# Unrolling the expert loop, a shorter threshold search and a reordered last tile in a Hyena/retention/expert-choice layer kernel

## The reference, cut to what matters here

```python
def trunk_layer(x, mod, p, s0_f, s0_b, use_rope):
    sh1, sc1, g1, sh2, sc2, g2 = mod
    h = rmsnorm(x, p["norm1_g"]) * (1.0 + sc1) + sh1
    out, s_f, s_b = mixer(h, p, s0_f, s0_b, use_rope)   # ends with merged @ w_out
    x = x + g1 * out
    h = rmsnorm(x, p["norm2_g"]) * (1.0 + sc2) + sh2
    x = x + g2 * ec_moe(h, p)
    return x, s_f, s_b

def ec_moe(h, p):
    xt = h.reshape(T, D)
    aff = softmax(xt @ p["w_router"])                   # 16 experts
    cap = (2 * T) // N_EXPERTS
    vals, idx = lax.top_k(aff.T, cap)                   # each expert takes its tokens
    xs = xt[idx]
    hid = silu(xs @ w_e_gate) * (xs @ w_e_up)
    ye = (hid @ w_e_down) * vals[..., None]
    return zeros.at[idx].add(ye)
```

## Time and profile before

| what | value |
|---|---|
| runs, median (lowest to highest) | 3529.71 us (3528.85 to 3532.29), 3 runs |
| the profiled execution, its own time | 3532.37 us |
| its span, first to last instruction | 3530.5 us |
| mean granted TensorE clock | 0.949 of full |
| busy: TensorE / VectorE / ScalarE / GpSimd | 91% / 46% / 36% / 10% |
| output phase's last row done | about 2091 us after the start |
| threshold search | about 2100 to 2155 us |
| experts on TensorE | about 2195 to 3510 us |

### The profile page before, as it was taken

One profiled execution on the slowest core, in us unless ns is written; L12 is line 12 of the kernel. 1 busy time (PEld: TensorE's weight loads), 2 busy tenths in 40 slices (PEclk: granted clock), 3 DMA queues, 4 the chain that ended last, 5 costly groups with the idle time before them and its releaser, 6 DMA issues. The chain is left out here.

```text
span 3530.5 us, 53171 instructions
## 1 busy us (share of the span) xinstructions
PE 3219.0 (91%) x19287; PEld 2754.7 (78%) x19287; DVE 1614.5 (46%) x3031; ACT 1283.2 (36%) x1955; POOL 356.0 (10%) x313
## 2 busy tenths in 40 slices
PE   7589999799889699999979963999999999999996
PEld 2278888789745689989978852989888889888995
DVE  5333232433346442323225546655555555555555
ACT  4544443323233031222124431444444444434445
POOL 1011111000034100000000001011111111111112
PEclk9799999899999799999999975999999999999998
DMA  8533332422299751422134431455555555555557
GB/s 336 194 118 101 114 112 84 142 64 66 67 348 353 237 181 56 130 93 96 55 128 149 159 135 61 162 204 190 177 190 181 177 173 169 169 170 182 200 204 279
DMA packets 281627, 565.64 MB, mean 160 GB/s; under 512 B 22296, under 2 KB 161432, under 8 KB 277289
## 3 DMA queue, kind: packets, MB, share of 16 engines
q1 hardware_dynamic: 257023, 503.83, 40.8%
q0 software_dynamic: 15456, 54.88, 5.3%
q10 hardware_dynamic: 8976, 4.46, 0.4%
HBM read 434.44 MB, written 128.64 MB: 159 GB/s over the span
## 5 line engine op out<-in xcount | busy, mean ns | idle before, releaser
L71 PE MATMUL experts_bank<-experts_xT_high,experts_w_high_gu 128*128 128x272 f32 x2048 | 604.3, 295 | 20.1 <-issue 15.0
L73 PE MATMUL experts_bank<-experts_xT_high,experts_w_low_gu 128*128 128x272 f32 x2048 | 596.4, 291 | 0.0
L72 PE MATMUL experts_bank<-experts_xT_low,experts_w_high_gu 128*128 128x272 f32 x2048 | 592.6, 289 | 0.0
L71 PEld LDWEIGHTS experts_bank<-experts_xT_high,experts_w_high_gu 128*128 128x128 f32 x2048 | 388.8, 190 | 33.4 <-issue 27.3
L72 PEld LDWEIGHTS experts_bank<-experts_xT_low,experts_w_high_gu 128*128 128x128 f32 x2048 | 389.9, 190 | 4.3
L73 PEld LDWEIGHTS experts_bank<-experts_xT_high,experts_w_low_gu 128*128 128x128 f32 x2048 | 389.0, 190 | 0.0
L2858 DVE TENSOR_TENSOR experts_w_low_gu<-experts_w_raw_gu,experts_w_high_gu 128x1024 fp32r<-128x1024 f32 x256 | 303.3, 1220 | 20.4 <-ACT experts_w_high_gu L2664 20.3
L2664 ACT ACTIVATE experts_w_high_gu<-experts_w_raw_gu 128x1024 fp32r<-128x1024 f32 x256 | 257.6, 1047 | 19.0 <-DMA experts_w_raw_gu<-in_w_stream 18.8
L71 PE MATMUL merge_pg<-merge_hT_high,merge_w_gates_high 128*128 128x436 f32 (+1 forms) x640 | 231.8, 362 | 13.2 <-DVE merge_hT_low L2015 13.2
L72 PE MATMUL merge_pg<-merge_hT_low,merge_w_gates_high 128*128 128x436 f32 (+1 forms) x640 | 231.3, 361 | 0.0
L73 PE MATMUL merge_pg<-merge_hT_high,merge_w_gates_low 128*128 128x436 f32 (+1 forms) x640 | 230.9, 361 | 0.0
(11 more groups left out here) (383 smaller groups left out, 6534.1 us busy)
## 6 DMA issues: line engine op xcount, KB each, us to landing
experts_w_raw_gu<-in_w_stream SPq DMA_DIRECT2D x256, 512.0 KB
experts_w_raw_d<-in_w_stream SPq DMA_DIRECT2D x128, 512.0 KB, 6.5
filters_wm<-in_w_mod SPq DMA_DIRECT2D x12, 2048.0 KB, 11.9
merge_hT<-scratch_hT SPq DMA_DIRECT2D x32, 436.0 KB, 6.7
scratch_h<-out_row SPq DMA_DIRECT2D x17, 520.0 KB, 2.7
tokens_x<-in_xs SPq DMA_DIRECT2D x17, 512.0 KB, 5.2
scratch_hT<-tokens_hT SPq DMA_DIRECT2D x17, 512.0 KB, 4.4
scratch_qkT<-tokens_qkT SPq DMA_DIRECT2D x17, 512.0 KB, 2.8
```

Of the source, the lines that this page charges most:

```text
L71: pe.matmul(out, lhs[0], rhs[0], start=start, stop=False)
L72: pe.matmul(out, lhs[0], rhs[1], start=False, stop=False)
L73: return pe.matmul(out, lhs[1], rhs[0], start=False, stop=stop)
```

## The change

Three parts. (1) In `experts` the loop is gone: all 16 experts are written out on TensorE, ScalarE, VectorE and GpSimd. (2) In the search the next candidates are formed from the step itself, beside the threshold and not behind it; the three counts over 16 elements become one comparison of 48 elements and one reduction; shifting the bits is moved behind the counts; TensorE waits only for `seg`, and VectorE's wait for the other constants is moved behind the search. (3) In the output phase the last tiles have another order: tile 16's gate product and residual sum are moved ahead of tile 15's copy on VectorE, its norm ahead of tile 14's softmax on ScalarE and VectorE; `pr` has a bank for each parity, so that router t waits for the exponential of t-2; tile 16 has a row slot of its own. Inside the loop of the output phase the order is the same as before. The diff, cut:

```diff
-        row = sb("row", [P, 2, ROW])
+        row = sb("row", [P, 3, ROW])
...
-        pr = pb("pr", [P, NE])
+        pr = pb("pr", [P, 2, 512])
...
-        VB = counted("dve_rows", ["t1", "x", "rstd", "h2a", "h2", "hT"])
+        VA, VB = counted("dve_sums", ["t1", "x"]), counted("dve_rows", ["rstd", "h2a", "h2", "hT"])
...
+        def slot(t, h):
+            return 2 if isinstance(t, int) and t == NT - 1 else h
...
                 def router(t, h):
                     pe.wait_ge(VB.sem, VB.at(t, "hT"))
                     pe.wait_ge(AB.sem, AB.at(t, "hT"))
-                    pe.wait_ge(AR.sem, AR.at(t - 1, "ex"))
+                    pe.wait_ge(AR.sem, AR.at(t - 2, "ex"))
...
-                for t in range(LOOP, NT):
-                    if t + 2 < NT:
-                        front(t + 2, t % 2, (t + 2) // 2)
-                    router(t, t % 2)
-                    if t + 1 < NT:
-                        turn(t + 1, (t + 1) % 2)
+                front(NT - 1, 0, (NT - 1) // 2)
+                router(NT - 3, 0)
+                turn(NT - 2, 1)
+                router(NT - 2, 1)
+                turn(NT - 1, 0)
+                router(NT - 1, 0)
...
             @block.scalar
-                for t in range(LOOP + 1, NT + 1):
-                    if t < NT:
-                        back(t, t % 2, t // 2, t + 2 < NT)
-                    router(t - 1, (t - 1) % 2)
+                norm(NT - 2, 1)
+                turned(NT - 2, 1)
+                norm(NT - 1, 0)
+                router(NT - 3, 0)
+                router(NT - 2, 1)
+                turned(NT - 1, 0)
+                router(NT - 1, 0)
...
             @block.vector
-                for t in range(LOOP + 1, NT + 1):
-                    if t < NT:
-                        back(t, t % 2, t // 2, int(t == NLAT), t + 2 < NT)
-                    router(t - 1, (t - 1) % 2)
+                last, k = NT - 1, (NT - 1) // 2
+                total(last - 1, 1, k - 1, 0)
+                norm(last - 1, 1, k - 1, 0)
+                total(last, 0, k, 1)
+                turned(last - 1, 1)
+                largest(last - 2, 0)
+                norm(last, 0, k, 1)
+                router(last - 2, 0)
+                largest(last - 1, 1)
+                router(last - 1, 1)
+                turned(last, 0)
+                largest(last, 0)
+                router(last, 0)
...
         def experts(eng, body):
-            with eng.Fori(0, LOOP // 2, 1) as i:
-                for h in range(2):
-                    body(i * 2 + h, h, i, True, True)
-            for e in range(LOOP, NE):
+            for e in range(NE):
                 body(e, e % 2, e // 2, e + 1 < NE, e + 2 < NE)
...
-                for dst, src in ((seg, d["seg"]), (caps[:], d["caps"]), (slot[:], d["slot"])):
+                sp.dma_start(seg, d["seg"]).then_inc(lds, 16)
+                for dst, src in ((caps[:], d["caps"]), (slot[:], d["slot"])):
                     sp.dma_start(dst, src).then_inc(ldc, 16)
...
-                pe.wait_ge(ldc, 80)
+                pe.wait_ge(lds, 16)
...
                 for j in range(3):
+                    v.memset(cand[:, :, j:j + 1], (j + 1) << (2 * DIGITS - 2))
                     mm = v.memset(bit[:, :, j:j + 1], (j + 1) << (2 * DIGITS - 2))
                 mm.then_inc(*R0.inc("bit"))
                 v.wait_ge(R0.sem, R0.at(0, "bit"))
-                v.wait_ge(ldc, 80)
...
                 for i in range(DIGITS):
+                    v.wait_ge(RB.sem, RB.at(i - 1, "cand"))
+                    v.tensor_tensor(reach, few[:].unsqueeze(1).broadcast_to([P, 3, CCAP]),
+                                    cand[:, 1, :].bitcast(F32).unsqueeze(2).broadcast_to([P, 3, CCAP]), ALU.is_ge)\
+                     .then_inc(*RB.inc("few"))
+                    for j in range(3):
+                        v.tensor_scalar(passing[j], flat_l, cand[:, 0, j:j + 1].bitcast(F32), 0.0, ALU.is_ge, ALU.add,
+                                        accum_out=cnt[:, j:j + 1])
+                    v.wait_ge(RB.sem, RB.at(i, "few"))
+                    v.tensor_reduce(cnt[:, 3:6], reach, mybir.AxisListType.X, ALU.add).then_inc(*RB.inc("count"))
+                    v.tensor_single_scalar(bit[:], bit[:], 2, ALU.logical_shift_right).then_inc(*RB.inc("bit"))
                     v.wait_ge(RB.sem, RB.at(i - 1, "thr"))
-                    v.tensor_tensor(cand[:], thr[:].unsqueeze(2).broadcast_to([P, 2, 3]), bit[:], ALU.bitwise_or)\
-                     .then_inc(*RB.inc("cand"))
-                    v.wait_ge(RB.sem, RB.at(i, "cand"))
-                    v.tensor_single_scalar(bit[:], bit[:], 2, ALU.logical_shift_right).then_inc(*RB.inc("bit"))
-                    for n, src in enumerate((flat_l, few[:])):
-                        for j in range(3):
-                            mm = v.tensor_scalar(passing[n][j], src, cand[:, n, j:j + 1].bitcast(F32), 0.0, ALU.is_ge, ALU.add,
-                                                 accum_out=cnt[:, 3 * n + j:3 * n + j + 1])
-                    mm.then_inc(*RB.inc("count"))
+                    v.wait_ge(RB.sem, RB.at(i, "bit"))
+                    v.tensor_tensor(rest[:], thr[:].unsqueeze(2).broadcast_to([P, 2, 3]), bit[:], ALU.bitwise_or)\
+                     .then_inc(*RB.inc("next"))
                     v.wait_ge(QB.sem, QB.at(i, "sum"))
...
                     v.wait_ge(RB.sem, RB.at(i, "step"))
+                    v.tensor_tensor(cand[:], step[:].unsqueeze(2).broadcast_to([P, 2, 3]), rest[:], ALU.bitwise_or)\
+                     .then_inc(*RB.inc("cand"))
                     v.tensor_tensor(thr[:], thr[:], step[:], ALU.bitwise_or).then_inc(*RB.inc("thr"))
                 v.wait_ge(RB.sem, RB.at(DIGITS - 1, "thr"))
+                v.wait_ge(ldc, 64)
```

More of the change, by code:

```diff
@@ L2159, in store_row @@
                     sp.wait_ge(VR.sem, VR.at(t, "row"))
-                    sp.dma_start(d["h2"][take(at, P), :], row[:, h, :]).then_inc(rst[h], 16)
+                    sp.dma_start(d["h2"][take(at, P), :], row[:, slot(t, h), :]).then_inc(rst[h], 16)
                 load(0, 0, 0)
@@ L2251, in front, with norm @@
                                    mT[:, h].rearrange("p a b -> p (a b)"), ACT.Copy).then_inc(*AF.inc("high"))
-                def back(t, h, k, more):
-                    act.wait_ge(VB.sem, VB.at(t, "x"))
+                def norm(t, h):
+                    act.wait_ge(VA.sem, VA.at(t, "x"))
                     act.activation(junk[:], x[:, h, :], ACT.Square, scale=DM ** -0.5, accum_out=ssq[:, h:h + 1])\
@@ L2258, in back, with turned @@
                     act.activation(ssq[:, h:h + 1], ssq[:, h:h + 1], ACT.Sqrt, bias=eps[:]).then_inc(*AB.inc("std"))
-                    if more:
-                        front(t + 2, h, k + 1)
+                def turned(t, h):
                     act.wait_ge(PB.sem, PB.at(t, "hT"))
@@ L2275, in _ @@
                 front(1, 1, 0)
-                back(0, 0, 0, True)
+                norm(0, 0)
+                front(2, 0, 1)
+                turned(0, 0)
                 with act.Fori(0, LOOP // 2, 1) as i:
                     for h in range(2):
-                        back(i * 2 + (h + 1), 1 - h, i + h, True)
+                        norm(i * 2 + (h + 1), 1 - h)
+                        front(i * 2 + (h + 3), 1 - h, i + h + 1)
+                        turned(i * 2 + (h + 1), 1 - h)
                         router(i * 2 + h, h)
-                for t in range(LOOP + 1, NT + 1):
-                    if t < NT:
-                        back(t, t % 2, t // 2, t + 2 < NT)
-                    router(t - 1, (t - 1) % 2)
+                norm(NT - 2, 1)
[5 more added lines that the diff above has]
+                router(NT - 1, 0)
             @block.vector
             def _(v):
+                VA.give(v)
                 VB.give(v)
@@ L2390, in phase_experts @@
         bit = sb("bit", [P, 2, 3], I32)
+        rest = sb("rest", [P, 2, 3], I32)
         cnt = sb("cnt", [P, 6])
@@ L2426, in phase_experts @@
         spread = ye[:].rearrange("p a b -> p (a b)")[:, 17 * P:18 * P]
-        passing = [[ye[:].rearrange("p a b -> p (a b)")[:, w[j]:w[j] + n] for j in range(3)]
-                   for w, n in (((18 * P, 20 * P, 22 * P), 2 * P), ((9 * P, 10 * P, 11 * P), CCAP))]
+        passing = [ye[:].rearrange("p a b -> p (a b)")[:, w:w + 2 * P] for w in (18 * P, 20 * P, 22 * P)]
+        reach = ye[:].rearrange("p a b -> p (a b)")[:, 9 * P:9 * P + 3 * CCAP].rearrange("p (a b) -> p a b", a=3)
         seg = ye[:].rearrange("p a b -> p (a b)")[:, 15 * P:17 * P]
@@ L2442, in phase_experts @@
         R0 = counted("dve_arrange", ["zero", "a0", "a1", "ac", "as", "prob", "few", "thr", "bit"])
-        RB = counted("dve_bits", ["cand", "bit", "count", "ml", "mc", "step", "thr"])
+        RB = counted("dve_bits", ["few", "count", "bit", "next", "ml", "mc", "step", "cand", "thr"])
         R1 = counted("dve_slots", ["gl", "gc", "need", "tl", "tc", "s0", "s1", "e0", "e1", "lim", "k0", "k1",
```

50 lines of the change are left out of this document (29 added, 21 removed).

## The result

The changed kernel takes 3488.53 us (median of 4 runs, 3487.38 to 3490.41), the kernel before 3531.0 us beside it (4 runs, 3528.85 to 3534.14): a ratio of 0.9877, 95% interval 0.9864 to 0.9889. The forecast was 3489.3 us. The profiled execution took 3487.38 us, its span is 3485.6 us, 44.9 less than the span before. The gain is 42.5 us by the medians and 43.4 us by the ratio.

The account below looks back on a forecast made before the run. TensorE, busy 91% of the span, was taken as the bound. Expert loop 19.9, search 12.8 and output phase's end 7.7 sum to 40.4 us, giving 3489.3 us from the 3529.71 median; range 3482 to 3499 us.

Parts of the forecast that it names:

- loop exit as straight code without a cost: Expert loop: expert 14, already written out, showed no idle time, so all 19.9 us of six round ends were taken.
- simpler waits: Expert loop: waits on constants without registers could give another 1 us, the bound of -21 us.
- all 80.26 us long: Sign for the expert loop: every stretch between experts' last products would have this length.
- The start: Routing search: TensorE waits for `seg` alone, so the first count comes at 2100.0 rather than 2104.55, -4.5 us.
- The round: Routing search: each round of the dependent chain would shrink by 0.57 us, from 3.38 to 2.81 us.
- first count to TensorE's product, 1.88 us: Search round: one reduction of 48 elements replaces three short counts with read-outs, -0.42 us.
- The two instructions that the trace did not show: Search round: the 48-element comparison delays the count by 0.12 us; the 48-element reduction takes 0.20 us.
- worked out by the rule: Search: if VectorE always waits for the empty pipe, the comparison delays the count by about 0.2 us; part worth 11.6 us.
- The wait for the exponential: Output phase's end: with two banks, router 16 no longer waits for tile 15's exponential, 1.7 us gone.
- The softmax of tiles 14 and 15: Output phase's end: on VectorE it would finish before the turned tile 16 arrives, with 0.4 us to spare.
- keep its clock through router 16: Output phase's end: TensorE, idling less, might still be at full clock there; the bound of -9.5 us.
- slower rival: Expert loop: each straight-code packet makes TensorE wait 2.3 us, 161 us more, time 3650 us; chance 3%.

Follow-up runs that it names:

- loop_only: Kernel before with only the experts written out on all four engines, search and output phase as before; ratio 0.9947.
- pe_straight: Kernel before with only TensorE's experts written out; ScalarE, VectorE and GpSimd keep their loops; ratio 0.9937.
- pe_looped: Kernel before with ScalarE's, VectorE's and GpSimd's experts written out; TensorE alone keeps the loop; ratio 0.9993.
- four_a_round: Kernel before with four experts in a loop round, three rounds, and four experts written out; 3519.5 us in one run.
- banks_only: Kernel before with only the two banks of `pr` in the output phase, order of the last tiles unchanged; 3530.05 us in one run.
- end_only: Kernel before with only the output phase's last tiles in the changed kernel's order, `phase_out` of the change; ratio 0.9982.
- loop_kept: Changed kernel with the expert loop put back, so search and output-phase edits alone; 3513.03 us.
- rest_only: Kernel before with one unused tile, `rest`, added where the change allocates it, moving later tiles by 32 bytes; ratio 0.9999.
- search_only: Kernel before with only the change's edits in the routing search, the added tile `rest` among them; ratio 0.9961.

## Why the prediction was right

**Part 1** (19.9 forecast, 23.8 in the stretches). The mechanism and the 19.9 us stand: loop_only has no long stretch, and pe_straight and pe_looped show that TensorE's loop alone makes them. The reading of the loop exit as straight code without a cost held for 13 experts. The extra 3.9 us (13 x 0.28 and 0.29) are not the "simpler waits" for which the step kept 1 us: loop_only has them and gains nothing by them. They come from part 2's added tile, so from a side of the change that the sum did not have. Of the signs that the forecast named, "all 80.26 us long" was therefore missed (79.98). The Trainium skill, "Runtime: NRT & Kernel Launch", section "Instruction fetch mechanics", says that instructions are prefetched in sequence and that a taken branch out of the fetched window stops the engine until its target is there. Where the gaps stand in four_a_round and pe_straight agrees with it; the fetch itself no run here isolates.

**Part 2** (12.8 forecast, 11.6 measured). The start was right: from the memset of `thr` to the first count there are 0.29 us, before 4.84, so 4.5 us less. The round fell from 3.38 to 2.90 us, not to 2.81. The step that was mis-sized is "first count to TensorE's product, 1.88 us", taken from round 0; in the next round of the same trace the product stands at 2109.78 and the count at 2107.99, 1.79. The new one takes 1.45 as forecast, so the gain is 0.34 and not 0.42. The two instructions that the trace did not show came out as taken: 0.13 (0.12 forecast) ahead of the first count, and the reduction 0.20 long. The comparison, 0.21 long, delays the count by 0.13, so the next operation does start while it runs. The Trainium skill, "VectorE: DVE Perf Modes", section "The DRAIN you can't avoid", has the next one wait for the empty pipe, but adds that one which is not held starts earlier; for this pair the trace agrees with the addition only. That the 11.6 us worked out by the rule equal the measured ones is chance: the rule's delay is not in the trace, and the 0.08 that the rounds lack lie in the count's term.

**Part 3** (7.7 forecast, 7.9 measured). Tile 16's turn starts 4.79 us after tile 15's copy, before 11.03: 6.2 for 6.0. The wait for the exponential gave 1.64 for 1.7, alone (banks_only) as together. The softmax of tiles 14 and 15 did end before the turned tile, at 2075.70 against 2076.17: 0.5 us to spare, 0.4 forecast. TensorE did not keep its clock through router 16: it took 3.60 us at a granted clock of 0.50, before 3.56 at 0.50.

**The sum.** 19.9 + 12.8 + 7.7 = 40.4 forecast. The parts measured alone give 18.7 + 13.8 + 6.4 = 38.9 us, the change as a whole 43.4 (0.0123 x 3531), with an interval of about 4 on each side. In the traces the parts give 23.8 + 11.6 + 7.9 = 43.3. The rest of 44.9 lies in stretches that vary between executions. Tile 14's copy starts 1.2 us earlier, where the 14 traces have it anywhere from 2054.2 to 2060.2 us. The first expert's gather is 1.2 us shorter. A small constant takes 3.43 us to land and not 1.54, for which VectorE waits 0.89 us; of the other traces only banks_only has that.

The forecast time is 0.8 us from the measured one, and some of that is luck. The gain was forecast 2.1 us too small (40.4 for 42.5 by the medians), and the kernel before came out 1.3 us slower in the comparison than the 3529.71 that the forecast started from. Within the gain, 3.9 us that the sum did not have stand against 1.2 us that part 2 lacks. Expert 0's first product moved by 20.9 us, where the forecast's sign was 20.5, but the varying stretches above are in it. The slower rival, code that starves TensorE, needed 0.58 us a packet; the stretches are all busy, so it is zero.

## What to carry to other kernels

Here the hardware loop cost the bounding engine, TensorE, 2.4 to 5.6 us at the end of each round but the last and nothing at its exit, and only that engine's loop had to be written out. Longer rounds bring a part of it: with four experts in a round two ends are left of six, and one run was 13.9 us faster. When an edit adds even a small tile (32 bytes a partition here, worth 0.28 us in 80.26), compare the length of untouched stretches before and after: the operands' addresses move, and a gain or a loss by that is not the edit's. Read a repeating chain's terms from a middle round, not from the first.

## What the runs showed that was not expected

- Products of 128 x 128 weights by 272 columns ran at two speeds, by where the tokens lie against the weights: 80.26 against 79.98 us an expert, of which 384 are such products, with one distance and with one that is 32 bytes longer. The down products of 512 columns, whose operands changed their distance too in the changed kernel, took the same time (22.69 and 22.72 us from start to start in expert 3 of the two traces). What in the engine or the memory makes it stays open, and other distances were not tried.
- The cost of the six round ends differs from trace to trace: 19.9 us in the kernel before, 20.2 in end_only, 21.4 in banks_only, 23.4 in loop_kept, 24.1 in pe_looped, 24.3 in rest_only and 24.9 in search_only. The idle time ahead of the next expert's first product hardly differs: 2.3 to 2.9 us at each end, 15.0 us for the six of the kernel before and 14.9 for those of search_only. What differs is the clock. The stretch's granted clock is 0.98 at three of the six ends of the kernel before and at all six of search_only and rest_only, and those ends cost another 1.3 to 1.6 us (one in search_only 2.4). The dearest, 5.6 us in pe_looped, has 0.96. Two ends at full clock are long by a second idle gap, 1.20 us in loop_kept and 0.52 in four_a_round. Why the clock falls behind some of the ends and not behind others stays open: the place of the data does not decide it alone, since pe_looped has the tiles of the kernel before, and with one trace for each kernel the spread between executions cannot be told from the kernel's share.
